# A convolution as block-Toeplitz matmuls on data reshuffled through DRAM, in a hybrid mixer and FFN trunk

## The chip, the cores and the metric

The kernel runs on the 8 cores of one Trainium2 chip. Each core takes 2 of the 16 sequences and runs both layers and the final norm on them alone; the weights are the same on all cores and no core talks to another. The time is the device time of the slowest core, in microseconds (us).

## The reference, cut to what matters

```python
# x: (16, 2048, 1024) f32; DA = DB = 384, DC = 256, CONV_WIDTH = 31, CHUNK = 128, D_FF = 2816
for l in range(2):
    h = rms_norm(x, norm1_g[l])
    z = h @ w_in[l]                                   # 1792 columns: a|gate (768), u|v (768), pool (256)
    # A: GLU, causal depthwise convolution over 31 positions, LayerNorm, silu, pointwise
    y = a * sigmoid(gate)
    y = depthwise_conv(y, conv_w[l]) + conv_b[l]      # left padding of 30
    ya = silu(layer_norm(y, conv_ln_g[l], conv_ln_b[l])) @ w_pw[l]
    # B: gated mixing of positions inside chunks of 128, 4 heads of 96 channels
    u, v = split(gelu(z_uv)); v = layer_norm(v)
    yb = u * (tril(w_s[l]) @ v + b_s[l])
    # C: trailing means over 2, 4, 8, 16 positions, minus the token, 64x64 map per group, scale
    yc = (trailing_mean(z_c, w) - z_c) @ w_pool[l] * pool_scale[l]
    x = x + concat(ya, yb, yc) @ w_out[l]
    h = rms_norm(x, norm2_g[l])
    x = x + (silu(h @ w_gate) * (h @ w_up)) @ w_down[l]
return rms_norm(x, final_g)
```

## The kernel before

The residual stream of a sequence stays in SBUF as xT, channels on partitions: 8 tiles of 128 channels by 2048 positions, f32. Work goes in four blocks j of 512 positions. Every operation is recorded by helpers of `Prog` (`mm` L343, `mms`, `transposes`, `act_op` L370, `tt` L386, `ts` L390, `stt` L397), so in the profile a line is that of a helper and a group is known by its tiles. Each engine executes its list in the order of recording and waits on semaphores where a tile's last writer or reader is on another engine.

A layer has two stages. In the **mixer**, `fa(j)` broadcasts the RMSNorm factor: `bcast_tok` (L484) makes four diagonal matrices on VectorE and multiplies ones by them in f32, and `rms_scale` (L496) writes hT, the normalised input in bf16. `fb1` and `fb2` project hT with w_in, mostly with channels on partitions, v with tokens on partitions. The convolution is split by taps: 18 taps are matmuls with diagonal matrices (`conv_pe`, 3 channel tiles times 18, each 512 columns), 6 taps are scaled by ScalarE and added by TensorE through an identity matmul, 6 are VectorE multiply-adds into acc and one a ScalarE scaling (`tap`, `tap30`). `lnv_stats` and `lnv_apply` normalise v, `pool_branch` does the trailing sums on VectorE, and the four 96-channel heads of the gating are matmuls of 128 columns. LayerNorm of the convolution takes its sums by matmuls with ones and two f32 broadcasts. The output projection (8 by 9 matmuls of 512 columns per block) is interleaved by hand with the next block's taps. `rms_tok_stats` (L460) squares on ScalarE and sums by one-column matmuls.

In the **FFN** the 22 hidden tiles go in chunks of 6, 6, 6, 4: gate and up projections from a ring of three weight slots, silu and product, then the down projection added to xT; the last chunk runs block by block and the statistics of a block are recorded after the next block's matmuls. Weights are cast from f32 to bf16 by DMAs of POOL's queue (`load_mixer_w1`, `load_mixer_wout`, `load_ring`, `load_wd`). SBUF is in regions, and `new_phase` makes all users of a region wait for all earlier ones. Between the sequences `fin_store` transposes and stores the output (four staging tiles) and `x_tr` transposes the next input.

## Time and profile before

| | us |
|---|---|
| median of 3 runs (lowest, highest) | 3571.84 (3571.19, 3571.9) |
| span of the profiled execution, slowest core | 3568.6 |
| shortest span among the 8 cores | 3562.7 |
| TensorE busy in that span | 3203.5 |
| VectorE (DVE) busy | 1693.4 |
| ScalarE (ACT) busy | 948.4 |
| GpSimd (POOL) busy | 205.0 |

The profiled execution's own time is taken as its span plus what lies around the span; the median of the runs is 3.2 us above the span. Busy time is the union of an engine's instructions. Matmuls are pipelined, so the mean duration of one (379 ns for 512 columns) is longer than the distance between two. The granted clock is the share of TensorE's full clock (2.4 GHz) that it was given in a stretch. The spans of the eight cores lie within 6 us of each other.

### The profile page before, as it was taken

To read this page: it belongs to the slowest core of one execution; us is meant where nothing else is said; L and a number is where in the kernel's file an instruction comes from. 1 tells how busy PE (TensorE), PEld (TensorE's weight loads), DVE (VectorE), ACT (ScalarE), POOL (GpSimd) and SP (SyncE) were. 2 spreads that over 40 slices of the span, in tenths; PEclk is the share of its full clock that TensorE was granted. 3 is DMA by queue.
4 is the path that set the end of the run, shared out by engine and by line. 5 is a ranking of instruction groups with operands and counts; after the bars stand their busy time and mean duration, and the time that the engine had idled before them with its cause. 6 is when DMAs were issued, how large, how long until landed. Compare 5 with 4: busy or idle time off the path is not lost.

```text
span 3568.6 us, 46876 instructions; the slowest of 8 cores (3562.7 to 3568.6 us)
## 1 busy us (share of the span) xinstructions
PE 3203.5 (90%) x15945; PEld 1564.1 (44%) x15945; DVE 1693.4 (47%) x3002; ACT 948.4 (27%) x1568; POOL 205.0 (6%) x253
## 2 busy tenths in 40 slices
PE   3799799999889879999969996999997897899997
PEld 3344344444444434444454443444443443444444
DVE  1667543323577653233356775223336765433235
ACT  3345310011344511100234552110114454101102
POOL 1000110000000010000000001000000000100000
PEclk7799889999889979999978996999997998899998
DMA  8000082120100063221150004522101000522202
GB/s 169 6 1 1 12 117 42 24 42 13 27 1 1 1 87 47 42 42 24 54 175 1 1 1 63 78 42 31 23 15 24 1 1 1 69 38 36 42 12 101
DMA packets 144642, 134.73 MB, mean 38 GB/s; under 512 B 4896, under 2 KB 120220, under 8 KB 144412
## 3 DMA queue, kind: packets, MB, share of 16 engines
q0 software_dynamic: 131008, 93.60, 19.2%
q1 hardware_dynamic: 13404, 38.14, 3.1%
q8 instruction: 135, 2.21, 0.2%
q14 instruction: 95, 0.78, 0.1%
HBM read 208.53 MB, written 16.78 MB: 63 GB/s over the span
## 4 chain that ended last, share of the span: by engine, by line
PE 80%; DVE 9%; issue 4%; ACT 4%; DMA 3%; DVEq 0%; SPq 0%; POOL 0%; ACTq 0%; POOLq 0%
PE bank L348 78%; DVE h2T L399 2%; ACT sqr_56 L377 2%; PE bank L366 1%; DVE hT L399 1%; DVE sA L387 1%; DVE acc L399 1%; PE bank L475 1%; DMA vst<-norm_g 1%; ACT sqb L377 0%; DMA out<-ostage_95 0%; DVE acc L387 0%; DVE sB L387 0%; DVE dg_60 L393 0%; ACT accb L377 0%
## 5 line engine op out<-in xcount | busy, mean ns | idle before, releaser
L348 PE MATMUL bank<-act,wd 128*128 128x512 bf16 x2816 | 632.4, 388 | 0.0
L387 DVE TENSOR_TENSOR xT<-xT,bank 128x512 f32<-128x512 f32 x640 | 439.6, 688 | 376.0 <-PE bank L348 369.0
L348 PE MATMUL bank<-h2T,ring_72 128*128 128x512 bf16 x2048 | 460.8, 388 | 31.5 <-DVE h2T L399 31.5
L348 PE MATMUL bank<-h2T,ring_73 128*128 128x512 bf16 x2048 | 444.6, 379 | 0.0
L348 PEld LDWEIGHTS bank<-act,wd 128*128 128x128 bf16 x2816 | 280.2, 100 | 345.9 <-issue 27.5
L348 PE MATMUL bank<-hT,w_in_sb 128*128 128x512 bf16 (+1 forms) x1536 | 364.6, 400 | 35.3 <-DVE hT L399 17.1
L377 ACT ACTIVATE sA<-bank 128x512 f32<-128x512 f32 x176 | 105.1, 597 | 1093.5 <-PE bank L348 1085.9
L387 DVE TENSOR_TENSOR act<-sB,bank 128x512 bf16<-128x512 f32 x176 | 121.1, 688 | 477.6 <-PE bank L348 477.6
L387 DVE TENSOR_TENSOR act<-sA,bank 128x512 bf16<-128x512 f32 x176 | 121.1, 688 | 469.3 <-PE bank L348 469.3
L348 PE MATMUL bank<-h2T,ring_74 128*128 128x512 bf16 x1536 | 333.5, 379 | 0.0
L348 PEld LDWEIGHTS bank<-h2T,ring_72 128*128 128x128 bf16 x2048 | 203.0, 100 | 286.6 <-issue 56.5
L348 PEld LDWEIGHTS bank<-h2T,ring_73 128*128 128x128 bf16 x2048 | 200.4, 98 | 241.6
L348 PEld LDWEIGHTS bank<-hT,w_in_sb 128*128 128x128 bf16 (+1 forms) x1536 | 172.0, 113 | 216.4 <-issue 66.5
L377 ACT ACTIVATE sB<-bank 128x512 f32<-128x512 f32 x176 | 105.1, 597 | 510.4 <-PE bank L348 510.4
L348 PEld LDWEIGHTS bank<-h2T,ring_74 128*128 128x128 bf16 x1536 | 150.3, 98 | 181.3
L377 ACT ACTIVATE sqr_55<-xT 128x512 bf16<-128x512 f32 x160 | 100.5, 628 | 241.6 <-PE bank L475 216.2
L348 PE MATMUL bank<-yb,wo_b 96*128 96x512 bf16 x512 | 131.6, 378 | 3.6 <-ACT ya L377 3.6
L348 PE MATMUL bank<-dg_60,onesF 128*128 128x128 f32 x256 | 76.7, 392 | 64.5 <-DVE dg_60 L393 50.3
L377 ACT ACT_TABLE_LOAD x48 | 61.6, 1283 | 259.5 <-DVE sA L387 98.4
L348 PE MATMUL bank<-ya,wo_a 128*128 128x512 bf16 x384 | 103.6, 378 | 0.0
L399 DVE SCALAR_TENSOR_TENSOR acc<-ybuf,cwT,acc 128x512 f32<-128x512 bf16 x144 | 98.9, 750 | 9.4 <-ACT acc L377 9.1
L399 DVE SCALAR_TENSOR_TENSOR acc<-ybuf_83,cwT,acc 128x512 f32<-128x512 bf16 x144 | 100.6, 750 | 4.7 <-ACT acc L377 4.6
(422 smaller groups left out, 3274.7 us busy)
## 6 DMA issues: line engine op xcount, KB each, us to landing
wd<-w_down POOLq DMA_DIRECT2D x12, 1536.0 KB, 12.1
ring_72<-w_gate_up POOLq DMA_DIRECT2D x32, 512.0 KB, 7.8
ring_73<-w_gate_up POOLq DMA_DIRECT2D x32, 512.0 KB, 7.4
w_in_sb<-w_in POOLq DMA_DIRECT2D x16, 768.0 KB, 41.3
ring_74<-w_gate_up POOLq DMA_DIRECT2D x24, 512.0 KB, 7.6
wd<-w_down POOLq DMA_DIRECT2D x4, 1024.0 KB, 8.4
out<-ostage_95 SPq DMA_DIRECT2D x8, 512.0 KB
out<-ostage_96 SPq DMA_DIRECT2D x8, 512.0 KB
```

What stands on the lines that cost most here:

```text
L348: ins = e.matmul(out, l, r, start=(first and i == 0), stop=(last and i == n - 1))
L366: ins = e.transpose(out, in_, idn)
L377: return e.activation(out=out, in_=in_, func=func, **kw)
L387: return P.add(eng, lambda e, out=out, in0=in0, in1=in1, op=op: e.tensor_tensor(out=out, in0=in0, in1=in1, op=op), reads=reads, writes=writes)
L399: e.scalar_tensor_tensor(out=out, in0=in0, scalar=scalar, in1=in1, op0=op0, op1=op1),
L475: ins = e.matmul(out, l, r, start=(k == 0 and out is mmg[0][0]), stop=(k == 7), skip_group_check=True)
```

## The change

The FFN's arithmetic stays. In the mixer and around it:

- The input of the projections is xb = x * norm1_g in bf16, without the RMSNorm factor. The projections of a, gate, u and v have tokens on partitions (384 columns each), and the factor, now one number per partition, is the scale of the operation that evicts the bank. Only the pooling branch has channels on partitions and multiplies by a broadcast factor.
- Broadcasts split the f32 factor into three bf16 parts and use three bf16 matmuls of 512 columns with ones (`split_bcast_closures`); the f32 ones go.
- The GLU output y is written to a DRAM buffer per block and read back as y2: partition (i, t) holds channel i of a group of 8 at position t of a block of 16 positions; the 128 blocks and the 48 groups lie on the free axis. The convolution is, per group of 8 channels, three matmuls of 128 columns with `toep`, the banded Toeplitz weights of the eight channels, which are expanded on the chip from `conv_t`. LayerNorm is then per partition (`lna_closures`), and f32 transposes bring the result back (`lnt`).
- In Z the window sums run on POOL, one channel tile after the other, each with a ScalarE copy of 64 partitions. The gating multiplies in 384-column matmuls, and `TR` transposes its result so that the output projection has 8 row blocks instead of 9.
- Closures for norms and LayerNorm are queued (`push`) and recorded a piece at a time (`tick`) between matmul groups, in the FFN too: there norm2 and the next layer's norm1 are recorded between the matmuls. `need` records the rest of a queue at once.
- SBUF tiles carry byte ranges instead of regions; a tile waits only for overlapping ones. The host lays out the weights and packs all vectors in one tensor, so the parameter transposes at the start go. SP has 24 DMA semaphores instead of 12.
- The final store and the next sequence's transposes are interleaved with its GLU projections; output staging has 3, then 2 tiles, and 8 at the very end.

```diff
+NI = 8
+NG = DA // NI
+ND = 3
+TB = 16
...
+    yd = [nc.dram_tensor("yd%d" % i, [S, DA], BF16, kind="Internal").ap() for i in range(2)]
...
+    def push(fn, tag=None, q=None):
+        (bg if q is None else q).append((fn, tag))
+    def pop(q):
+        fn, tag = q.popleft()
+        fn()
+        if tag is not None:
+            done.add(tag)
+    def tick(n=1):
+        for _ in range(n):
+            if bg:
+                pop(bg)
+            elif lo:
+                pop(lo)
...
+    def split_bcast_closures(s, l, j, rt, kind, sink):
+        br = B("r", kind, j)
+        bs = B("spl")
+        bd = B("dsp")
+        def split():
+            c = slice(4 * j, 4 * j + 4)
+            vec(lambda e: e.tensor_copy(out=spb[:, 0, :], in_=rt[:, c]), [br], [bs])
+            tt(spf[:, 0:4], rt[:, c], spb[:, 0, :], ALU.subtract, [br, bs], [bs])
+            vec(lambda e: e.tensor_copy(out=spb[:, 1, :], in_=spf[:, 0:4]), [bs], [bs])
+            tt(spf[:, 4:8], spf[:, 0:4], spb[:, 1, :], ALU.subtract, [bs], [bs])
+            vec(lambda e: e.tensor_copy(out=spb[:, 2, :], in_=spf[:, 4:8]), [bs], [bs])
+        def dia(i):
+            for q in range(4):
+                ts(dsp[:, i, q, :], identb[:], spb[:, i, q:q + 1], None, ALU.mult, None, [bs, bC], [bd])
+        def bc():
+            bk, bb = next_bank()
+            mm(bk[:], [(onesb[:], dsp[:, i].rearrange("p q t -> p (q t)")) for i in range(3)], [bd, bC], [bb])
+            sink(bk, bb)
+        push(split)
+        push(lambda: dia(0))
+        def dia12():
+            dia(1)
+            dia(2)
+        push(dia12)
+        push(bc, (kind + "bc", s, l, j))
...
+    def A(s, l, j):
+        need(("r1", s, l, j))
+        yt = ytok[j % 2]
+        for q in range(4):
+            tc_ = slice(q * 128, (q + 1) * 128)
+            rc = r1[:, 4 * j + q:4 * j + q + 1]
+            br = B("r", "r1", j)
+            rd = [bxb(j, k) for k in range(8)] + [w_a.b()]
+            bk, bb = next_bank()
+            mm(bk[:, 0:DA], [(xb[j][:, k, tc_], w_a[:, k, DA:2 * DA]) for k in range(8)], rd, [bb])
+            sg = sig[q % 2]
+            act_op(sg[:], bk[:, 0:DA], AF.Sigmoid, [bb, br], [sg.b()], scale=rc)
+            tick()
+            bk, bb = next_bank()
+            mm(bk[:, 0:DA], [(xb[j][:, k, tc_], w_a[:, k, 0:DA]) for k in range(8)], rd, [bb])
+            stt(yt[:, q, :], bk[:, 0:DA], rc, sg[:], ALU.mult, ALU.mult, [bb, br, sg.b()],
+                [yt.b(q, lo=768 * q, n=768)])
+            tick()
+        ydt = yd[s % 2]
+        byd = B("yd", s % 2, j)
+        dma("sync", ydt[j * NT:(j + 1) * NT, :].rearrange("(q p) c -> p q c", p=128), yt[:],
+            [yt.b(q, lo=768 * q, n=768) for q in range(4)], [byd])
+        src = ydt.rearrange("(b t) (i g) -> i t b g", t=TB, i=NI)
+        for i in range(NI):
+            dma("sync", y2[TB * i:TB * (i + 1), 2 + 32 * j:2 + 32 * (j + 1), :], src[i, :, 32 * j:32 * (j + 1), :],
+                [byd], [y2b(j)])
+    def toep_closures():
+        gs = NG // 3
+        for part in range(3):
+            for i in range(NI):
+                def f(part=part, i=i):
+                    o = toep[:, part * gs:(part + 1) * gs, :, i, :]
+                    v = vconv[:, part * gs:(part + 1) * gs, :, :]
+                    wr = [toep_b(b) for b in range(4 * part, 4 * part + 4)]
+                    if i % 2 == 0:
+                        ts(o, v, M8[:, i:i + 1], None, ALU.mult, None, [vconv.b(), bC], wr)
+                    else:
+                        act_op(o, v, AF.Copy, [vconv.b(), bC], wr, scale=M8[:, i:i + 1])
+                push(f, None, lo)
+    def conv():
+        for b in range(12):
+            bk, bb = next_bank()
+            groups = []
+            for gp in range(4):
+                g = 4 * b + gp
+                groups.append((bk[:, gp * 128:(gp + 1) * 128],
+                               [(y2[:, 2 - d:2 - d + NBLK, g], toep[:, g, d].rearrange("p i t -> p (i t)"))
+                                for d in range(ND)]))
+            mms(groups, [y2b(u) for u in range(-1, NJ)] + [toep_b(b)], [bb])
+            tt(xc[:, 32 * b:32 * b + 32, :], bk[:].rearrange("p (c t) -> p c t", t=TB),
+               cbB[:, 32 * b:32 * b + 32].unsqueeze(2).to_broadcast([128, 32, TB]),
+               ALU.add, [bb, cbB.b()], [xc_b(b)])
+            tick()
+    def lna_closures(s, l):
+        bst = [B("bna", i) for i in range(4)]
+        allx = [xc_b(b) for b in range(12)]
+        def stats(t):
+            tq, ti = t // 4, t % 4
+            vec(lambda e: e.bn_stats(out=bna[:, ti, 0:6], in_=xc[:, :, t]), allx, [bst[ti]])
+            vec(lambda e: e.bn_aggr(out=bna[:, ti, 8:10], in_=bna[:, ti, 0:6]), [bst[ti]], [bst[ti]])
...
+        def app(t):
+            ti = t % 4
+            ts(xc[:, :, t], xc[:, :, t], bna[:, ti, 8:9], bna[:, ti, 10:11], ALU.subtract, ALU.mult,
+               [bst[ti]] + allx, [B("xh", t)])
+        for tq in range(4):
+            for ti in range(4):
+                push(lambda t=4 * tq + ti: stats(t), None, lo)
+            push(fin, None, lo)
+            for ti in range(4):
+                push(lambda t=4 * tq + ti: app(t), ("lna", s, l, tq) if ti == 3 else None, lo)
+    def lnt(s, l, tq):
+        need_lo(("lna", s, l, tq))
+        for ct in range(3):
+            bk, bb = next_bank()
+            transposes([(bk[:, ti * 128:(ti + 1) * 128], xc[:, ct * 128:(ct + 1) * 128, 4 * tq + ti], identF[:])
+                        for ti in range(4)], [B("xh", 4 * tq + ti) for ti in range(4)] + [xc_b(b) for b in range(12)] + [bC],
+                       [bb])
+            dst = silT[:, ct, :].rearrange("p (b t) -> p t b", t=TB)[:, 4 * tq:4 * tq + 4, :]
+            act_op(dst, bk[:].rearrange("p (t b) -> p t b", t=4), AF.Silu, [bb, bPV],
+                   [silT.b(ct, tq, lo=4096 * ct, n=4096)], scale=pvc(l, PV_LNG + ct), bias=pvc(l, PV_LNB + ct))
+            tick()
+    def V(s, l, j):
+        rd = [bxb(j, k) for k in range(8)] + [w_uv.b()]
+        br = B("r", "r1", j)
+        for q in range(4):
+            bk, bb = next_bank()
+            mm(bk[:, 0:DB], [(xb[j][:, k, q * 128:(q + 1) * 128], w_uv[:, k, DB:2 * DB]) for k in range(8)], rd, [bb])
+            act_op(vg[:, q, :], bk[:, 0:DB], AF.Gelu, [bb, br], [vg.b(q, lo=1536 * q, n=1536)],
+                   scale=r1[:, 4 * j + q:4 * j + q + 1])
+            tick()
...
+    def SP(s, l, j):
+        for h in range(4):
+            hc = slice(96 * h, 96 * h + 96)
+            bk, bb = next_bank()
+            mm(bk[:, 0:DB].rearrange("p (q d) -> p q d", q=4), [(wsT[:, h, :], vn[:, :, hc])],
+               [vn.b(q, lo=768 * q, n=768) for q in range(4)] + [B("wsT")], [bb])
+            stt(ybt[:, :, hc], bk[:, 0:DB].rearrange("p (q d) -> p q d", q=4), pvc(l, PV_BS + h), ug[:, :, hc],
+                ALU.add, ALU.mult, [bb, bPV] + [ug.b(q, lo=768 * q, n=768) for q in range(4)], [ybt.b()])
...
+    def Zprep(s, l, j):
+        def sink(bk, bb):
+            act_op(rbc[:], bk[:], AF.Copy, [bb], [rbc.b()])
+        split_bcast_closures(s, l, j, r1, "r1", sink)
+    def Z(s, l, j):
+        need(("r1bc", s, l, j))
+        rd = [bxb(j, k) for k in range(8)] + [w_z.b()]
+        if j == 0:
+            pool(lambda e: e.memset(zc[:, :, 0:ZH], 0.0), [], [zc.b()])
+        else:
+            act_op(zc[:, :, 0:ZH], zc[:, :, NT:NT + ZH], AF.Copy, [zc.b()], [zc.b()])
+        for m in range(2):
+            bk, bb = next_bank()
+            mm(bk[:], [(w_z[:, k, m * 128:(m + 1) * 128], xb[j][:, k, :]) for k in range(8)], rd, [bb])
+            tt(zc[:, m, ZH:ZH + NT], bk[:], rbc[:], ALU.mult, [bb, rbc.b()], [zc.b()])
+            tick()
+        W = ZH + NT
+        for m in range(2):
+            zm = zc[:, m, :]
+            tt(zG[:, 1:W], zm[:, 1:W], zm[:, 0:W - 1], ALU.add, [zc.b()], [zG.b()], eng="gpsimd")
+            tt(zF[:, 3:W], zG[:, 3:W], zG[:, 1:W - 2], ALU.add, [zG.b()], [zF.b()], eng="gpsimd")
+            if m == 1:
+                tt(zG[:, 7:W], zF[:, 7:W], zF[:, 3:W - 4], ALU.add, [zF.b()], [zG.b()], eng="gpsimd")
+                tt(zF[:, 15:W], zG[:, 15:W], zG[:, 7:W - 8], ALU.add, [zG.b()], [zF.b()], eng="gpsimd")
+            act_op(zF[0:64, ZH:W], zG[0:64, ZH:W], AF.Copy, [zG.b()], [zF.b()])
+            stt(pp[:, m, :], zF[:, ZH:W], invw[:, m:m + 1], zm[:, ZH:W], ALU.mult, ALU.subtract,
+                [zF.b(), zc.b(), bC], [pp.b()])
...
+            dma("sync", sgB[:, 0, :], sg_ln_g_d[l].partition_broadcast(128), [], [sgB.b()])
+            dma("sync", sgB[:, 1, :], sg_ln_b_d[l].partition_broadcast(128), [], [sgB.b()])
+            dma("sync", cbB[:], conv_b_d[l].partition_broadcast(128), [], [cbB.b()])
+            pool(lambda e: e.memset(y2[:, 0:2, :], 0.0), [], [y2b(-1)])
+            need(("r1", s, l, 3))
+            toep_closures()
+            A(s, l, 3)
+            drain()
+            load_wo(l, 0)
+            load_wo(l, 1)
+            V(s, l, 0)
+            U(s, l, 0)
+            conv()
+            lna_closures(s, l)
+            Zprep(s, l, 0)
+            SP(s, l, 0)
+            V(s, l, 1)
+            Z(s, l, 0)
+            Zprep(s, l, 1)
+            TR(s, l, 0)
+            U(s, l, 1)
+            PM(s, l, 0)
+            SP(s, l, 1)
+            V(s, l, 2)
...
+            V(s, l, 3)
+            Z(s, l, 2)
+            Zprep(s, l, 3)
+            TR(s, l, 2)
+            U(s, l, 3)
+            PM(s, l, 2)
+            SP(s, l, 3)
+            lnt(s, l, 0)
+            Z(s, l, 3)
+            load_wo(l, 2)
+            TR(s, l, 3)
+            lnt(s, l, 1)
+            lnt(s, l, 2)
+            lnt(s, l, 3)
+            for fp in range(NRING):
+                load_ring(l, fp, fp)
+            PW(s, l, 0)
+            PM(s, l, 3)
+            load_wd(l, 0)
+            PW(s, l, 1)
+            for j in range(NJ):
+                WO(s, l, j)
+                norm2(s, l, j)
+                if j + 2 < NJ:
+                    PW(s, l, j + 2)
```

## Rows read from the trace of the kernel before

**Rows 1.** The page, busy time by engine and the chain's shares
```profile
PE 3203.5 (90%) x15945; PEld 1564.1 (44%) x15945; DVE 1693.4 (47%) x3002; ACT 948.4 (27%) x1568; POOL 205.0 (6%) x253
...
PE 80%; DVE 9%; issue 4%; ACT 4%; DMA 3%; DVEq 0%; SPq 0%; POOL 0%; ACTq 0%; POOLq 0%
```

**Rows 2.** Windows by stage: start:end, length, busy (instructions) per engine, clock, DMA share, GB/s
```profile
0.00:50.00 50.00, 27.14 (x218) 25.14 (x219) 11.55 (x22) 23.12 (x40) 8.11 (x21) 0.86 1.03 230
0.00:105.90 105.90, 35.00 (x277) 31.05 (x278) 21.93 (x48) 28.32 (x49) 16.07 (x33) 0.70 0.72 147
105.90:456.00 350.10, 302.54 (x1540) 153.65 (x1540) 233.87 (x462) 151.86 (x247) 24.28 (x27) 0.88 0.06 8
475.00:906.00 431.00, 431.00 (x1999) 195.38 (x1998) 134.63 (x196) 52.01 (x87) 18.00 (x22) 1.00 0.28 39
1779.00:1862.00 83.00, 53.41 (x465) 46.87 (x462) 43.25 (x74) 34.93 (x62) 8.41 (x11) 0.75 0.65 195
2210.00:2689.00 479.00, 469.62 (x2188) 211.88 (x2188) 164.87 (x243) 63.67 (x108) 20.03 (x24) 0.98 0.30 42
2689.00:2707.00 18.00, 6.75 (x68) 5.04 (x66) 7.34 (x18) 6.98 (x13) 4.43 (x7) 0.54 0.36 54
3533.00:3568.60 35.60, 21.64 (x176) 18.03 (x176) 23.05 (x34) 6.15 (x12) 2.01 (x2) 0.80 0.60 245
```

**Rows 3.** The chain that ended last, in time: start, length, what
```profile
81.92 1.25 DMA vst<-pool_scale
...
89.55 4.12 DMA wsst<-w_s
...
271.53 1.02 POOL bnst_63 L652
...
354.56 31.94 PE bank L348 x147
...
1805.19 15.85 DMA out<-ostage_95
```

**Rows 4.** Groups of instructions, first mixer: shapes, count | busy us, mean ns | idle before
```profile
L348 PE MATMUL bank<-w_in_sb,hT 128*128 128x384 bf16 x128 | 21.5, 326 | 0.0
...
L348 PE MATMUL bank<-sqb,identb 128*128 128x512 bf16 x36 | 13.6, 419 | 0.9 <-ACT sqb L377 0.7
```

**Rows 5.** Small matmuls: group of the whole span, timeline, group of the first mixer
```profile
L475 PE MATMUL bank<-ocS,sqr_55 128*128 128x1 bf16 x640 | 38.5, 164 | 65.0 <-ACT sqr_55 L377 63.2 <-DVE rtok L393 1.8
...
1837.76 0.71 PE L366 MATMUL bank<-ident,xT 128*128 128x128 f32 x5
...
L358 PE MATMUL bank<-wsT,vn 128*96 128x128 bf16 x64 | 8.9, 314 | 2.6 <-DVE acc L387 2.6
```

**Rows 6.** Groups of DVE and ACT, first mixer
```profile
L399 DVE SCALAR_TENSOR_TENSOR acc<-ybuf_83,cwT,acc 128x512 f32<-128x512 bf16 x36 | 25.1, 750 | 1.2 <-ACT acc L377 1.1
...
L387 DVE TENSOR_TENSOR xT<-xT,bank 128x512 f32<-128x512 f32 x32 | 21.8, 688 | 23.7 <-PE bank L348 22.5 <-PE bank L475 1.3
...
L377 ACT ACTIVATE sqr_55<-xT 128x512 bf16<-128x512 f32 x16 | 10.0, 627 | 29.0 <-PE bank L475 25.3 <-DVE xT L387 3.7
...
L399 DVE SCALAR_TENSOR_TENSOR vg<-vg,bnst_63,sgB 128x384 f32<-128x384 f32 x16 | 9.8, 613 | 5.1 <-POOL bnst_63 L652 5.1
...
L646 DVE BATCH_NORM_STATS2 bnst_62<-vg 128x6 f32<-128x384 f32 x16 | 8.9, 559 | 4.0 <-ACT vg L377 3.0
...
L377 ACT ACTIVATE sil<-sA,pv 128x512 bf16<-128x512 f32 x8 | 6.5, 814 | 3.4 <-DVE sA L387 3.3
```

**Rows 7.** DMA queues of the page (packets, MB, share of 16 engines); groups of POOL
```profile
q0 software_dynamic: 131008, 93.60, 19.2%
q1 hardware_dynamic: 13404, 38.14, 3.1%
...
L412 POOL TENSOR_SCALAR_AFFINE_SELECT ident<-onesF 128x128 f32<-128x128 f32 x1 | 0.3, 292 | 0.2 <-POOL onesF L411 0.2
...
L416 POOL MEMSET mhalf<- 128x16 f32 x1 | 0.1, 111 | 0.1
```

More of the change, by code:

```diff
@@ L1 @@
+from collections import deque
 import numpy as np
@@ L55 @@
 SEM_LIMIT = 30000
[L56 removed]
+N_DMA_SEMS = {"gpsimd": 20, "sync": 24, "scalar": 4}
 class Prog:
```

1111 lines of the change are left out of this document (492 added, 619 removed).

## The prediction

> **What bounds the kernel now.** I read the page first: TensorE (PE) is busy 90% of the span and carries 80% of the chain that ended last [rows 1]. That share averages two kinds of stage, so I cut the span at the first and last matmul of each [rows 2]. An FFN stage takes 479 us (the others are within 2 of it); in its middle TensorE is busy in 431.0 of 431.0 us at clock 1.00, 1999 recorded matmuls, 0.216 us each. A mixer stage takes 350 us (the others within 2), TensorE busy in 302.5 at clock 0.88: the granted clock is at the lower of its levels (1.2 GHz) for about a quarter of the time, after idle stretches. The start (105.9), the gaps from FFN to mixer (83 between the sequences, 18 inside the second, and 19.5 inside the first, what the rest of the span leaves) and the last store (35.6) make up the 3568.6.
>
> Inside a mixer the chain is trains of up to 32 us of matmuls, cut by pieces like the POOL power of 1.02 us for which DVE and then TensorE stand [rows 3]. So TensorE bounds the mixer, with holes where another engine must deliver. At 0.216 us per 512 columns the convolution is 3*18*4 = 216 diagonal matmuls (46.7 us) plus the 72 identity ones that add ScalarE's taps (36 of them 13.6 us, so 27) [rows 4]: 73 of the 302 us.
>
> **The change, priced per layer.** I build the new stage times instead of subtracting, because the order of work is new throughout.
>
> *GLU projections A(0..3).* 4*4*2*8 = 256 matmuls of 384 columns at 21.5/128 = 0.168 [rows 4]: 43 us, plus one block of statistics (32 at 38.5/640 = 0.060 [rows 5]), 45. DVE has per block 4 multiplies of 384 (0.62 each) and 4 of the scalings that replace hT; ScalarE 4 sigmoids, 8 squares, 4 scalings at about 0.6 [rows 6]: both under TensorE's 11 us per block. rstd is now needed by the eviction only, so the matmuls no longer wait for statistics, power, broadcast and scaling; the holes before a mixer [rows 2] go. If this cover failed, up to the 18 us of such a gap would return.
>
> *V(0), U(0)*: 64*0.168 = 11.
>
> *Reshuffle.* Each block is written to DRAM and read back by 8 DMAs on SP in pieces of 48 bf16, 96 bytes: 512 tokens * 8 = 4096 pieces, 256 for each of 16 DMA engines. No row shows such a piece. Software-queue packets average 19.2% of 16*3568.6 over 131008 = 0.084 us (714 bytes), hardware-queue ones 3.1% over 13404 = 0.13 us (2.8 KB) [rows 7]; the load of w_s (512 packets of 512 bytes, 32 per engine) holds the chain for 4.12 us against 1.25 for one of a few packets [rows 3]: (4.12-1.25)/32 = 0.09. A piece cannot be below zero; bounds 0 to 0.13. I take 0.045, half the 512-byte row, since a fifth of the bytes and the same overhead are left. Four blocks need 1024 pieces per engine and begin 14 us into the stage; the convolution is ready at 45+11 = 56. 14+46, and 4 for the last write and receipt (1.25 for a small load, two of them and the gaps), is 64: wait 8. At 0 there is none, at 0.13 it is 14+133+4-56 = 95. The Trainium skill, page "DMA: Bandwidth & Descriptors", section "Why small descriptors are slow (HBM only)", gives about 3 bus cycles of overhead beside one per 32 bytes; by that a piece is an estimated 0.01 us, there would be no wait and the sum be 32 us lower. No trace here shows it.
>
> *Convolution*: 48*3 = 144 matmuls of 128 columns, each with its own weight load. Nearest rows: 0.060 (load plus one column), f32 transposes of 128 columns (five in 0.71 with the last one's latency, so 0.106 to 0.14), the w_s matmuls 8.9/64 = 0.139 [rows 5]. Bounds 9 to 20, taken 0.10: 14. All of the 73 us of TensorE and of the tap work on DVE (72 at 0.69, 50 us [rows 6]) and ScalarE goes, so does the ybuf halo. The 24 expansions of the Toeplitz weights lie beside V(0) and U(0), 12 on each engine, 768 elements, at about the 0.7 to 0.8 of 512 f32 ones.
>
> *The V/Z/U/SP rounds.* TensorE needs V, U 192*0.168 = 32, Z 64*0.216 = 14, broadcasts 3, SP 3, bf16 transposes 48*0.106 = 5, pooling map 2: 58 for three and a bit rounds, plus 5 for the f32 transposes. DVE needs per round, by [rows 6]: V statistics and scaling 4*(0.559+0.182+0.613+0.618)+0.2+1.3 (wait for the power) = 9.4; SP 2.5; split and diagonals 0.8+3.0; Z two evictions and two differences 2.9; its part of the LayerNorm of the convolution (16 tokens of statistics 0.74 and normalisation 0.6, four powers: 27 in all, two thirds in three rounds) 6.1: 24.7. To it comes a chain in Z that the kernel before does not have: window sums on POOL (2, then 4 operations of 528 elements, f32), each set followed by a ScalarE copy, for which DVE stands with its next instruction in order; ScalarE stands too, with the evictions of U and TR behind it. POOL's 128-element one-input operation takes 0.292 against 0.111 for 16 elements [rows 7], 1.6 ns an element, so 0.95 for 528 with one input and at most double with two; I take 1.25 (bounds 0.95 to 1.9). 6*1.25 + 2*0.6 + crossings = 10.5, of which DVE works 2: 8.4 idle (bounds 6 to 12). The next V begins only after SP: 2.5 more, since TensorE with 16 of 35 us of work will be granted the lower clock much of the time, as at 2689 where it is busy 6.75 of 18.0 at 0.54 [rows 2]. A round: 24.7+8.4+2.5 = 35.6 (bounds 20, where TensorE sets it, and 45, where the clock stays low). Three rounds 107; the last Z, what is left of the normalisation (9) and 9 Silu evictions at 0.81 add 26. Together 133. The skill's page "GPSIMD Engine Reference", section 3.1, gives 2.6 cycles at 1.2 GHz for a two-input element, an estimated 1.14 us without overhead; the sum by it moves by less than 3 us per layer.
>
> *PW, WO.* 36+256+12 at 0.216 = 66, and 128 statistics at 0.060 = 8: 73 (8 row blocks instead of 9 saves 7). DVE in it: 32 adds at 0.688 and norm2 of three blocks at 10: 52; ScalarE 32 squares at 0.62: 20; both hidden. The loads of the last third of w_out and of the rings wait for Z(3) and the last transposes, issued 20 us or more before use, against 8 us to land by the page's list of DMA issues.
>
> *FFN.* 2112*0.216 = 456, 96 statistics now interleaved 6; the last block's norm2 is late by 8. 470 against 477 to 479.
>
> Layer: 45+11+8+14+133+73+470 = 754, four 3016.
>
> *Ends.* Start: the serial parameter loads, of which [rows 3] show the last but one and w_s, and their transposes go: they end at 94. A(0) needs two x blocks and w_a, 7.3 MB, at 230 GB/s [rows 2] 32 us; it then runs with 10 us of transposes between: 42 over a normal layer. Between sequences: 256 f32 transposes, 27 to 41 us by clock, and output tiles that are too few: the chain stands 15.85 us for one store [rows 3]. 60, much as before (62 more than an inner gap). End 31 (35.6 now).
>
> Sum 3016+42+60+31 = 3149, against the profiled span of 3568.6. The median of the runs, 3571.84, is 3.2 above that span, so 3152.
>
> **Rivals.**
> R1, the rounds are bound by TensorE: DVE's work spreads into neighbouring stages and POOL's chain is covered. For: DVE's average is only 47%. Against: in-order DVE stands for POOL. The 133 becomes 75: 3152-4*58 = 2920.
> R2, the 96-byte reads: at 0.084 each, 14+86+4-56 = 48 instead of 8: +160 = 3312; at 0.13, 95, +348 = 3500. For: it is the mean of the queue in this trace. Against: those packets are 7 times as large.
> R3, slower than before: the same reads at over 0.147 us a piece. 14+1024p+4-56 must exceed 8 by the 105 us per layer that the change gives (3571.84-3152 over 4); that is p = 0.147. At 0.2 the wait is 167, +636 = 3788. For: 96 bytes is far below anything measured here, 8 cores read at once. Against: every row is below 0.13.
> R4, the clock stays low and rounds cost 45: +28 a layer, with PW and the start of WO cold: 3152+4*32 = 3280.
> R5, the change does not do what it says (the Toeplitz or f32 transposes cost so much that the 73 us stay): 3152+4*55 = 3370. Against: column counts, and 0.106 us.
>
> **How the numbers follow.** Forecast 0.48, R4 0.14, R1 0.15, R2 0.14, R5 0.04, R3 0.05. A difference under 0.2% can't be told from none; no case lands there except a sliver between R2 and R3: 0.01. Faster 0.94, slower 0.05. The forecast's own range by the bounds of convolution, POOL and ends is 3080 to 3230; taking in R4, R1 and the lower half of R2: 2920 to 3370.
>
> **What would show it.** Mixer stages of about 285 us; A at clock 1.00 with TensorE 95% busy; the y2 reads landing about 12 us after issue (22 and more would be R2); in the rounds idle DVE before the pp operations, released by POOL or ScalarE, and TensorE idle before SP, released by DVE; POOL additions near 1.25 us; WO dense; FFN near 470. The forecast is wrong if the rounds show TensorE over 90% busy, if the convolution's first matmul waits over 30 us for DMA, or if WO or the FFN stops being dense because weights come late.

## The result: slower by 1.7%, and the profile after

The changed kernel takes 3630.5 us (3634.8 in a second run) beside 3571.6 for the kernel before on the same chip: ratio 1.0173, interval 1.0151 to 1.0195. My 3152 was 479 us too low, and the time lies above the range. (In some executions of either kernel one die is granted a lower clock and takes longer; such executions are left out everywhere.)

The page of after, its parts 1, 3 and 4, then the lines of part 5 that this document reads:
```profile
span 3628.2 us, 43607 instructions; the slowest of 8 cores (3613.8 to 3628.2 us)
...
PE 2787.5 (77%) x14864; PEld 1387.4 (38%) x14864; DVE 1384.3 (38%) x2657; ACT 820.5 (23%) x1240; POOL 276.7 (8%) x347
...
q1 hardware_dynamic: 87408, 49.59, 4.9%
...
PE 65%; DMA 12%; DVE 11%; issue 5%; POOL 4%; ACT 2%; DVEq 1%; SPq 0%; POOLq 0%; ACTq 0%
PE bank L326 62%; DMA y<-yd 8%; DVE dsp L371 3%; DMA yd<-ytok 2%; POOL zF L365 2%; ACT silT L355 1%; PE bank L336 1%; PE bank L344 1%; POOL zG L365 1%; DVE h2T L377 1%; DVE ybt L377 1%; DVE pp L377 1%; DVE vg L377 1%; DVE bnv L730 1%; DMA w_a_sb<-w_a 1%
...
L326 PE MATMUL bank<-dsp,onesb 128*128 128x512 bf16 x96 | 41.1, 558 | 355.3 <-DVE dsp L371 355.3
...
L336 PE MATMUL bank<-toep,y 128*128 128x128 bf16 x576 | 45.0, 253 | 196.1 <-DMA y<-yd 196.1
...
L355 ACT ACTIVATE silT<-bank,pv 128x512 bf16<-128x512 f32 x48 | 107.6, 2655 | 0.1
```
TensorE's busy time fell as planned, from 3203.5 to 2787.5 us against [rows 1], 416 less. The span grew by 60, so TensorE is idle 476 us more. The chain names the takers: DMA, 3% in [rows 1], has 12%, of which 8% are the reads of y2 (`y<-yd`), and POOL has 4%. The two releasers to look at first stand on the idle column: 355.3 us before the broadcast's matmuls (`dsp,onesb`) and 196.1 us before the convolution. 

The windows of one layer, in the columns of [rows 2], cut at A, V/U 0 and the wait, convolution, rounds with tail, PW/WO, the start of FFN, and the rest of FFN (the cut at 1321 lies 8 us inside the FFN, whose first matmul starts at 1312.5):
```profile
932.00:978.00 46.00, 44.68 (x323) 27.04 (x321) 15.45 (x31) 24.72 (x42) 2.17 (x3) 1.00 0.21 41
978.00:1045.00 67.00, 10.83 (x67) 6.31 (x65) 11.61 (x26) 13.22 (x18) 2.27 (x3) 0.60 0.34 60
1045.00:1056.30 11.30, 11.03 (x145) 11.03 (x146) 7.56 (x11) 0.00 (x0) 0.00 (x0) 0.81 0.01 1
1056.30:1227.30 171.00, 72.30 (x387) 40.99 (x385) 86.64 (x209) 58.88 (x66) 38.56 (x39) 0.70 0.06 9
1227.30:1321.00 93.70, 81.84 (x428) 36.20 (x428) 44.02 (x103) 22.86 (x40) 3.58 (x4) 0.91 0.23 41
1321.00:1360.00 39.00, 19.47 (x104) 8.53 (x105) 18.36 (x40) 6.79 (x12) 1.01 (x1) 0.78 0.00 1
1360.00:1777.00 417.00, 417.00 (x1926) 188.69 (x1925) 127.95 (x187) 50.22 (x84) 16.39 (x28) 1.00 0.26 48
```
A is as forecast. In the second window TensorE has 11 us of work in 67, in the fourth 72 in 171, with VectorE busy only 87: no engine is busy most of the time there, so waits set it; which, the experiments have to show.

The stages of all layers, cut at the first and last matmul of each in the trace (to about 2 us), summed over the four layers, beside my terms and the repaired kernel `e15_all_sp` (told below):

| us, whole program | forecast | after | error | e15_all_sp |
|---|---|---|---|---|
| A, four blocks | 180 | 179 | -1 | 179 |
| V/U 0 and wait for y2 | 76 | 238 | +162 | 67 |
| convolution | 56 | 44 | -12 | 51 |
| rounds and tail | 532 | 683 | +151 | 558 |
| PW, WO | 292 | 339 | +47 | 321 |
| FFN | 1880 | 1955 | +75 | 1897 |
| start (beyond a normal A) | 42 | 76 | +34 | 51 |
| between sequences | 60 | 84 | +24 | 73 |
| end | 31 | 30 | -1 | 29 |
| sum | 3149 | 3628 | +479 | 3226 |

**Why the convolution waits.** A stretch of the chain of waits (start, length, what) in the second window:
```profile
992.43 2.27 DMA y<-yd
994.73 0.04 issue
994.77 2.22 DMA y<-yd
...
997.44 2.58 DMA yd<-ytok
1000.05 0.03 issue
1000.08 2.21 DMA y<-yd
...
1016.94 3.44 DMA sgB<-sg_ln_g
...
1021.36 4.89 DMA yd<-ytok
1026.29 0.03 issue
1026.32 2.31 DMA y<-yd
...
1042.65 2.48 DMA y<-yd
1045.13 0.14 issue
1045.27 4.73 PE bank L336 x46
```
One read follows the other; each starts when the last has landed. In the code the eight reads of a block write eight different sets of 16 partitions but name one record, `y2b(j)`, and a writer waits for the record's last writer, here on SP. So far this is read off the code and the chain; e1 and e16 below test it. A block costs 2.6 to 4.9 us for its write and 8 times 2.2, about 20 in series, where A takes 11: the queue falls behind by 9 us a block.

**What a round is made of.** VectorE's order in the second round of the same layer (41 us, from one SP to the next); in brackets the idle time before the operation and what ended it:
```profile
1102.01 2.78 DVE L377 SCALAR_TENSOR_TENSOR ybt<-bank,pv,ug 128x384 bf16<-128x384 f32 x4 [5.09 <-PE bank L326]
...
1123.19 0.75 DVE L377 SCALAR_TENSOR_TENSOR pp<-zF,invw,zc 128x512 bf16<-128x512 f32 x1 [2.36 <-ACT zF L355]
...
1129.63 0.75 DVE L377 SCALAR_TENSOR_TENSOR pp<-zF,invw,zc 128x512 bf16<-128x512 f32 x1 [5.68 <-ACT zF L355]
...
1131.85 4.23 DVE L371 TENSOR_SCALAR dsp<-identb,spb 128x128 bf16<-128x128 bf16 x12
```
VectorE works 21.7 us of the 41. It stands 8.0 for ScalarE's copies, which follow POOL's sums, 5.0 for TensorE before it can evict the next SP's banks, 2.5 for two POOL powers, and 3.5 goes in gaps of less than 0.1 us between its 53 operations. TensorE's own 22 us of idle time before the broadcast lie beside this chain; they are its consequence.

### The profile page after: what moved, and what is told of

It is laid out like the page before. It is cut to its first block, busy times and chain, and to the rows that moved or that the text cites. A ratio compares the mean times of both kernels' runs of the same rounds, so it can differ in the third digit from the quotient of the medians.

```text
span 3628.2 us, 43607 instructions; the slowest of 8 cores (3613.8 to 3628.2 us)
## 1 busy us (share of the span) xinstructions
PE 2787.5 (77%) x14864; PEld 1387.4 (38%) x14864; DVE 1384.3 (38%) x2657; ACT 820.5 (23%) x1240; POOL 276.7 (8%) x347
## 3 DMA queue, kind: packets, MB, share of 16 engines
q1 hardware_dynamic: 87408, 49.59, 4.9%
## 4 chain that ended last, share of the span: by engine, by line
PE 65%; DMA 12%; DVE 11%; issue 5%; POOL 4%; ACT 2%; DVEq 1%; SPq 0%; POOLq 0%; ACTq 0%
PE bank L326 62%; DMA y<-yd 8%; DVE dsp L371 3%; DMA yd<-ytok 2%; POOL zF L365 2%; ACT silT L355 1%; PE bank L336 1%; PE bank L344 1%; POOL zG L365 1%; DVE h2T L377 1%; DVE ybt L377 1%; DVE pp L377 1%; DVE vg L377 1%; DVE bnv L730 1%; DMA w_a_sb<-w_a 1%
## 5 line engine op out<-in xcount | busy, mean ns | idle before, releaser
L326 PE MATMUL bank<-h2T,ring 128*128 128x512 bf16 x5632 | 1237.3, 383 | 39.4 <-DVE h2T L377 39.4
L326 PEld LDWEIGHTS bank<-h2T,ring 128*128 128x128 bf16 x5632 | 553.8, 99 | 718.4 <-issue 67.1
L365 DVE TENSOR_TENSOR act<-tsil,bank 128x512 bf16<-128x512 f32 x352 | 242.0, 688 | 973.7 <-PE bank L326 961.9
L355 ACT ACTIVATE tsil<-bank 128x512 f32<-128x512 f32 x352 | 210.1, 597 | 1588.6 <-PE bank L326 1585.5
L326 PE MATMUL bank<-dsp,onesb 128*128 128x512 bf16 x96 | 41.1, 558 | 355.3 <-DVE dsp L371 355.3
L355 ACT ACTIVATE sqr<-xT 128x512 bf16<-128x512 f32 x320 | 192.5, 623 | 205.1 <-PE bank L524 194.0
L336 PE MATMUL bank<-toep,y 128*128 128x128 bf16 x576 | 45.0, 253 | 196.1 <-DMA y<-yd 196.1
L326 PE MATMUL bank<-w_uv_sb,xb 128*128 128x384 bf16 x1024 | 193.3, 351 | 0.0
L326 PE MATMUL bank<-w_a_sb,xb 128*128 128x384 bf16 x1024 | 178.8, 331 | 1.7 <-DVE r L371 1.7
L326 PE MATMUL bank<-ya,wo 128*128 128x512 bf16 x384 | 112.9, 406 | 0.0
L326 PE MATMUL bank<-ybT,wo 128*128 128x512 bf16 x384 | 108.6, 393 | 0.0
L355 ACT ACTIVATE silT<-bank,pv 128x512 bf16<-128x512 f32 x48 | 107.6, 2655 | 0.1
```

The costliest lines, as they stand in the source:

```text
L326: ins = e.matmul(out, l, r, start=(first and i == 0), stop=(last and i == n - 1))
L336: ins = e.matmul(out, l, r, start=(i == 0), stop=(i == n - 1))
L355: return e.activation(out=out, in_=in_, func=func, **kw)
L365: return P.add(eng, lambda e, out=out, in0=in0, in1=in1, op=op: e.tensor_tensor(out=out, in0=in0, in1=in1, op=op), reads=reads, writes=writes)
```

## The experiments

Each is an edit of the changed kernel. Ratios are to the kernel before, run beside the experiment; "a layer" is the mean of the table's cuts.

**e1_reads_free.** The eight reads get records of their own.
```diff
-                [byd], [y2b(j)])
+                [byd], [y2b(j, i)])
```


> The eight reads of a block get a record of their own each, so that none waits for the one before; nothing else changes. Theory A (the reads stand in a row: each is issued when its forerunner has landed, 2.2 us a piece, 17 to 18 us a block, so the last block lands 88 us after the first is written and the convolution waits 56.4 us): the wait falls to under 10 us, the layer from 869 to about 820, between the sequences another 20 us go since the stores of the output stand behind the reads on SP, together 3630 to about 3410. Theory B (the 96-byte pieces themselves cost the time, my rival R2): a block still takes 17 us and the time stays within 1% of 3630.

3544.0, from one execution, so there is no interval. Its cores end at 3497 to 3543; the latest takes 505 us in each FFN for 489, with a granted clock of 0.81 over 60 us at its start, where TensorE is busy 19.8 or more of each 20. Why, no run here shows. Wait and V/U 0 are 22 to 27 us a layer for 47 to 67: the serial reads are the cause of most of that wait. Of the expectation (wait under 10, 3410) this falls short: the wait itself is still 12 to 17 us, and the gain is 87 us, 131 on the best core, not 220. What is left of the wait is mostly the write of the last block: it takes 11 to 14.5 us in the second layer, while the two loads of w_out recorded before it keep the DMA engines 94% busy, against a median of 3. In e15, where these loads come later, it has a median of 2.6 and the wait is 7. TensorE's wait before the broadcasts stays, 345.9 us.

**e2_reads_fat.** Reads stay serial, but each takes contiguous pieces of 3072 bytes, so y2's contents are in another order.
```diff
-            dma("sync", y2[...], src[i, :, 32 * j:32 * (j + 1), :],
+            dma("sync", y2[...].rearrange("p b g -> p (b g)"),
+                ydt[j * NT:(j + 1) * NT, :].rearrange("(i t r) c -> i t (r c)", i=NI, t=TB)[i],
```


> The eight reads of a block still wait for each other but move the same bytes in pieces of 3072 instead of 96 bytes; the convolution gets its input in a wrong order. Theory A: 2.0 to 2.2 us per read as before, wait of the convolution 50 us or more, time within 1% of 3630. Theory B: a read well under 2 us and a wait under 20 us, time 3500 or less.

3590.9 (one execution; 1.1% below 3630, where I had said within 1%); the wait with V/U 0 is still 42 to 58 us. The page's DMA line of after, of this and of e1 (KB each, median us from issue to landing):
```profile
y<-yd SPq DMA_DIRECT2D x128, 48.0 KB, 2.2
```
```profile
y<-yd SPq DMA_DIRECT2D x128, 48.0 KB, 1.8
```
```profile
y<-yd SPq DMA_DIRECT2D x128, 48.0 KB, 2.8
```
31 more pieces per DMA engine (512 pieces of 96 bytes against 16 of 3072, over 16 engines) cost 0.4 us of 2.2, so 0.013 us each; the rest is what a DMA of this size takes with long pieces too, paid eight times in series. Free of each other (third line) each takes longer, 2.8, but they overlap. So the piece was not the danger of my rivals R2 and R3.

**e3_sums_dve.** The window sums run on VectorE (`eng="gpsimd"` dropped in four places).

> The six window sums of Z per block go from POOL (1.07 to 1.3 us each) to DVE. Theory C (the chain POOL, ScalarE, DVE sets the rounds, crossings included): about 10.5 us of chain become 6 operations of 0.69 plus two ScalarE copies, 5 to 6 us less per block, 16 blocks, about 3550. Theory D (DVE's own work sets the rounds): 4 us more of it per block, 3630 to 3690.

3592.2 to 3597.6 (ratio to before 1.0062, 1.0045 to 1.0080): rounds and tail 161 a layer for 170. POOL's detour costs 9 us a layer, half of theory C and a quarter of the 38 a layer by which rounds and tail miss the forecast.

**e4_bcast_early.** The next block's broadcast is recorded whole behind Z's two evictions, ahead of the sums.
```diff
+        if j + 1 < NJ:
+            Zprep(s, l, j + 1)
+            need(("r1bc", s, l, j + 1))
         W = ZH + NT
```


> The split, the diagonals and the broadcast matmuls of block j+1 are recorded right after the evictions of Z(j), ahead of the window sums, instead of behind them. Theory E (TensorE stands 20 to 23 us per round at the broadcast matmuls in the middle of U because their diagonals are behind Z's chain in DVE's order, so U, PM, SP and V come late): the wait at the broadcast falls to about 5 us, DVE makes its 5.5 us of split and diagonals while POOL works, a round falls from 41.5 to about 34 us, three per layer, 3630 to about 3540. Theory D (DVE's sum of work sets the round): the wait moves to SP and the time falls by less than 30 us.

3620.9 to 3633.3 (ratio 1.0156, 1.0132 to 1.0179), rounds 168: 3 us a layer, although it attacks the largest line of the page. Both theories had the wait itself wrong, it stays where it was: TensorE still stands 57.1 us before the broadcasts in the second layer's rounds (68.9 in after), because V's statistics and scaling and Z's evictions stand ahead of the diagonals on VectorE, and new is a wait of 9.4 for ScalarE's `ybT`. VectorE still waits 2.95 and 5.69 us for the sums.

**e10_order.** Z(j), its evictions, POOL's sums and the next broadcast stand before V(j+1), `pp` after V's statistics; the second channel tile gets its own zF.
```diff
-            V(s, l, 1)
             Z(s, l, 0)
+            Zw1(s, l, 0)       # sums on POOL
             Zprep(s, l, 1)
+            V(s, l, 1)
+            Zw(s, l, 0)        # pp on VectorE
             TR(s, l, 0)
```


> Only the order of the rounds is changed: Z(j), its two evictions, the window sums on POOL (a second buffer zF for its second half) and the broadcast of r for the next block stand before V(j+1), pp after V(j+1)'s statistics. DVE's and POOL's work stays the same. Theory O: a round of 41.5 us is DVE's 24 us of work plus 17 us of waits in its order (POOL's sums before pp, TensorE's broadcast and evictions behind them); with the sums beside V's work the round falls to 28 to 33 us, rounds and tail from 171 to 130 to 140 a layer, and the time to 3470 to 3510. Rival C: the chain from V's matmul over its gelu, statistics, POOL's power, eight operations and SP's evictions is what sets the round, whatever stands between; it stays at 38 or more and the time at 3600 or more.

3551.8 to 3558.4 (ratio 0.9957, 0.9942 to 0.9973), below the kernel before; rounds and tail 151 a layer, 20 less. The work is the same, the order alone was worth 77 us (2.16% of 3571.6), half of what the optimistic theory said. A round takes 32 to 33 us: VectorE's waits for the sums (8.0) and for TensorE (5.0) are gone from it, and its busy time is 25.7 instead of 21.7 (why, under e20). The waits of TensorE (us in total, times, longest) of after, then of e10:
```profile
PE bank L326 <- DVE dsp L371: 355.3, 32, 23.0
```
```profile
PE bank L327 <- DVE dsp L372: 211.9, 32, 10.9
```

**e5_silt, e12_fours.** The Silu evictions of the convolution take 2.64 us each; I had 0.81. They write bf16 at a step of 32 bytes. e5 holds silT time-major, so that it is written contiguously and PW's matmuls read it with that step; e12 keeps the layout and turns the loops, to write runs of four.
```diff
-            dst = silT[...].rearrange("p (b t) -> p t b", t=TB)[:, 4 * tq:4 * tq + 4, :]
+            dst = silT[...].rearrange("p (t b) -> p t b", t=TB)[:, 4 * tq:4 * tq + 4, :]   # e5
+            dst = silT[...].rearrange("p (b t) -> p b t", t=TB)[:, :, 4 * tq:4 * tq + 4]   # e12
```


> The 12 silT evictions a layer write bf16 with a step of 32 bytes and take 2655 ns each (48 in the trace of after). Here they write contiguous runs of 128 (silT held time-major), and PW's matmuls read the strided view instead. Theory F: the time is the strided write; each falls to 0.7 to 0.9 us, ScalarE is freed 22 us a layer, the tail after the last round loses 10 to 15 of it a layer, and the time is 3570 to 3590. Rival G: the time is that of the strided PSUM source or of Silu itself; the evictions stay over 2 us and the time stays 3630. Rival H: the stride moves to TensorE, PW's 512-column matmuls grow from 0.23 to 0.4 us or more (36 a block of 512), which gives 10 to 25 us back a layer: 3630 or above.

> e5_silt moved the stride of 32 bytes from ScalarE's write (2642 ns, now 777) to TensorE's read (379 ns a matmul, now 1038) and cost 27 us a layer in PW. Here silT stays token-major, so PW reads contiguous columns again, and the eviction iterates block by block: it writes runs of four tokens (8 bytes, step 32) and reads PSUM with a step of 512 bytes. Theory: the cost of the eviction is that of each lone 2-byte write, so runs of four take 0.8 to 1.3 us, PW is back at 379 ns, the tail loses 8 to 14 us a layer and the time is 3575 to 3600. Rival: the read of PSUM with a step costs as much as the write did, the eviction stays at 2.6 us, and the time at 3630.

Instructions of tile silT (ns min/median/max) in after, e5 and e12:
```profile
L326 PE MATMUL bank<-silT,w_pw_sb x144: 379/379/634, 360.3 to 3072.8; 128*128 128x512 bf16 x144
L355 ACT ACTIVATE silT<-bank,pv x48: 2537/2642/2846, 320.1 to 3023.1; 128x512 bf16<-128x512 f32 x48
```
```profile
L326 PE MATMUL bank<-silT,w_pw_sb x144: 1017/1038/1044, 345.6 to 3154.7; 128*128 128x512 bf16 x144
L355 ACT ACTIVATE silT<-bank,pv x48: 767/777/794, 317.0 to 3085.2; 128x512 bf16<-128x512 f32 x48
```
```profile
L326 PE MATMUL bank<-silT,w_pw_sb x144: 379/379/634, 348.9 to 3023.0; 128*128 128x512 bf16 x144
L355 ACT ACTIVATE silT<-bank,pv x48: 769/777/787, 320.2 to 2975.9; 128x512 bf16<-128x512 f32 x48
```
e5: 3691.1 to 3742.1 (ratio 1.034, 1.0316 to 1.0365), 60 slower by the ratio: the step now slows 144 matmuls from 379 to 1038 ns, 26 us a layer in PW/WO, against 12 won in the tail. e12: 3582 to 3587 (ratio 1.0043, 1.0027 to 1.0059): 777 ns with runs of 8 bytes, PW as before. Reading PSUM at a step of 512 bytes costs nothing.

**e8_start.** Own records for the halves of w_a and w_uv, and the mask on wsT recorded before V(0).
```diff
-        dma("gpsimd", w_a[:, :, 0:DA], w_a_d[l, :, :, 0:DA], [], [w_a.b()])
+        dma("gpsimd", w_a[:, :, 0:DA], w_a_d[l, :, :, 0:DA], [], [w_a.b("SIB", 0)])
```


> The two halves of w_a and of w_uv get records of their own, so that POOL's queue does not wait for one half before it issues the other, and the mask on wsT is recorded just before V(0) instead of with the loads. Theory: the first norm power comes at 66 us in after because POOL stands behind these waits (24.4, 11.0 and 20.1 us in its queue); it now comes near 47, A of the first layer falls from 72 to about 52, and the time to about 3608. Rival: the first group waits for the bytes of w_a themselves, not for POOL's power; A of the first layer stays near 70 and the time at 3630.

3615.6 to 3620.2 (ratio 1.0135, 1.0115 to 1.0155), 14 less by the ratio, though the two intervals touch. The trace carries it: the first A starts 8 us earlier and takes 57 for 72, and 8 of this is given back in the wait for y2. Part of the forecast's +34 at the start.

**e18_bcast_cheap.** The broadcasts alone: 12 operations of 128 columns become 3 of 512, norm2's broadcast comes nine closures later, WO has four closures a tick instead of two.
```diff
-            for q in range(4):
-                ts(dsp[:, i, q, :], identb[:], spb[:, i, q:q + 1], None, ALU.mult, None, [bs, bC], [bd])
+            tt(dsp[:, i], identb[:].unsqueeze(1).to_broadcast([128, 4, 128]),
+               spb[:, i, :].unsqueeze(2).to_broadcast([128, 4, 128]), ALU.mult, [bs, bC], [bd])
...
-            tick(2)
+            tick(4)
```


> After with the broadcasts alone changed: the 12 diagonals as three operations of 512 columns, norm2's broadcast behind nine empty closures, four closures a tick in WO. Theory: what TensorE stands in WO and at the start of FFN (5.1, 5.1, 1.8 and then 7.3 and 5.6 us in one layer) goes, 10 to 15 us a layer from PW/WO and FFN together, nothing from the rounds: 3570 to 3590. Rival: VectorE's evictions of WO now wait behind the closures, PW/WO grows as FFN falls (as from e14_all_fours to e15_all_sp, +7 and -12): 3600 to 3615.

3520.5 and 3525.2 (ratio 0.9860, 0.9831 to 0.9889): some 108 less, twice my theory. FFN is 474 a layer for 489, PW/WO 80 for 85, and the rounds, from which I expected nothing, 162 for 170. The three parts of this edit were not separated. The large piece is FFN's start, where in after TensorE stood 7.3 us for `dsp` and 5.6 for h2T and had a clock of 0.78 in 39 us.

**All repairs.** e11_all has e1, e10, e5, e8, the cheap broadcast with nine closures and three a tick, sgB and cbB loaded ahead of the reads on SP, wo loaded after them. e13 has the old Silu eviction in its place, e14 that of e12; e15 is e14 with SP(j+1) ahead of PM(j) and four closures a tick.

> All repairs together: reads of a block free of each other, the order of the rounds of e10_order, silT written contiguous, the broadcast's 12 diagonals as three operations of 512 columns, the broadcast behind nine empty closures in WO with three a tick, own records for the weight halves, sgB and cbB loaded before the reads on SP, wo loaded after the reads. Theory (each term is a loss of its own place): -131 for the reads as the undisturbed cores of e1_reads_free had it, -120 for the rounds, -50 for silT, -25 for the broadcasts in WO and at the start of FFN, -20 for the start, sum 3280; range 3230 to 3340, below both kernels. Rival: the terms hide each other (freed ScalarE and VectorE time only moves the wait), and the kernel ends between 3400 and 3480.

> e11_all with silT evicted as in after (2-byte writes with a step of 32 bytes). PW/WO falls from the 101 to 105 us of e11_all to 80 to 84 a layer, as its 36 matmuls go from 1036 to 379 ns; the tail grows by the evictions, 8 to 13 us a layer. Theory that the two places add: 3393 - 4*22 + 4*10 = 3345. Rival, that ScalarE in the tail is now the bound (12 evictions of 2.64 us are 32 us): the tail grows by 20 or more and the time stays 3390.

> e11_all with the eviction of e12_fours. If runs of four are cheap (0.8 to 1.3 us): PW/WO at 80 to 84 us a layer and the rounds and tail at 138 as in e11_all, 3393 - 4*22 = 3305. If they cost 2.6 us, it equals e13_all_old_silu.

> e14_all_fours with SP(j+1) recorded ahead of PM(j), so that TensorE's stand for pp (14.1 us over the rounds of one layer in e11_all) lies behind the matmuls that DVE's next evictions wait for, and four closures a tick in WO, so that the last block's norm lies less in the first blocks of FFN (11.8 us for h2T and 5.4 for dsp there). Theory: -5 to -10 us a layer, 20 to 40 below e14_all_fours. Rival: pp and vn are ready within 3 us of each other on DVE, and closures run earlier only put DVE's work ahead of WO's evictions: within 10 us of e14_all_fours.

e11: 3393.2 (one execution), 113 above my sum; PW/WO at 102 to 106 a layer shows the largest part of why, e5's matmuls. e13: 3297.6 to 3299.3 (ratio 0.9240, 0.9226 to 0.9255), PW/WO 75 for 104, rounds 150 for 138: 64 less over four layers, which is what lies between it and the best cores of e11 (3362 in the profiled run). e14: 3239.3 and 3249.6, rounds 138, PW/WO 73. e13 and e14 came out 47 and some 60 below their expectations, which started from 3393 instead of 3362 and took 22 us a layer for the 29 to 31 of PW/WO. e15: 3225.2 to 3228.2 (ratio 0.9039, 0.9024 to 0.9053), some 17 below e14. The windows of e15's second layer (V/U 0, then convolution, rounds, PW/WO, FFN):
```profile
866.70:884.00 17.30, 10.56 (x68) 6.35 (x66) 6.22 (x15) 12.39 (x17) 0.00 (x0) 0.89 0.27 45
884.00:896.00 12.00, 10.90 (x144) 10.47 (x143) 9.69 (x20) 0.14 (x1) 2.21 (x4) 0.87 0.73 125
896.00:1036.40 140.40, 81.54 (x387) 43.42 (x387) 89.85 (x176) 39.13 (x66) 37.77 (x34) 0.75 0.03 5
1036.40:1116.20 79.80, 71.61 (x398) 32.78 (x397) 40.60 (x76) 21.92 (x39) 5.92 (x9) 0.97 0.38 60
1116.20:1590.70 474.50, 462.40 (x2226) 210.16 (x2224) 160.92 (x242) 69.12 (x115) 19.34 (x31) 0.99 0.29 49
```
The wait for the reads is gone (17.3 us with 10.6 of work; the other 6.7 are for ScalarE's U evictions, behind the Toeplitz expansions on that engine). In the rounds TensorE still works only 81.5 of 140.4 us.

**e16_all_serial, e17_reads_order.** e15 with the one record for the eight reads back; and after with only e1 and e10.

> e15_all_sp with one thing put back: the eight reads of a block write one record again, so that each waits until the one before has landed. Theory A (the serial reads are worth the same wherever they stand: last landing 17 to 20 us after the write of each block, the SP queue full over all four blocks of A): V0/U0 and the wait go from 15 to 17 us back to 45 to 65, and the time from 3227 to 3350 to 3400. Rival B (in e1_reads_free much of the gain was that the other loads no longer stood behind the reads on SP; with sgB and cbB ahead and wo behind, the serial reads cost less): 3290 or less.

> After with only two repairs, the free reads of e1_reads_free and the order of e10_order. If the two add, it takes off 131 (the undisturbed cores of e1_reads_free) and 79: 3630 - 131 - 79 = 3420, range 3405 to 3435. If the reads' landing and the rounds share a wait, 3450 or more.

e16: 3383.7 to 3395.3 (ratio 0.9483, 0.9454 to 0.9513): the serial reads alone cost 160 us, with the stage at 40 to 64 us a layer for 15 to 17. e17: 3433 to 3469 (ratio 0.9657, 0.9591 to 0.9722), where adding them gave 3405 to 3435. In its fastest run the cores end at 3394 to 3432, others at up to 3468, and single FFNs take 509 us for 491 as in e1. So the two roughly add; with this spread it can't be said more sharply.

**e19_all_tick4, e20_all_sums_dve.** e15 without the swap; and that with the window sums on VectorE.

> e14_all_fours with four closures a tick in WO and PM(j) left ahead of SP(j+1). In e15_all_sp both edits moved at once: rounds 138 to 139.5, PW/WO 72.3 to 79.8, FFN 486 to 474. If the tick did all of the gain, this stands 0 to 8 us below e15_all_sp (3219 to 3227); if the swap gave part of it, 5 or more above (over 3232).

> e19_all_tick4 with the ten window sums of a round... of a block (six operations of about 525 columns) on VectorE instead of POOL. In e3_sums_dve this gave 9.5 us a layer, since VectorE stood idle while POOL summed. In the new order VectorE works beside POOL, and both slow each other there (dsp 692 alone, 1.21 us beside POOL; POOL's sums 1.06 alone, 1.32 beside it). Theory 1 (VectorE is now the engine of the rounds): six operations more of 0.65 us are 3.9 us a round, rounds 138 to 148, time +30 to +45. Theory 2 (the mutual slowing costs more than it hides): the rounds stay at 138 or fall, time within 10.

e19: 3225.7 to 3257.1 (ratio 0.9072, 0.9032 to 0.9111). The times lie on both sides of my marks and decide nothing. The stages do: PW/WO and FFN together are 560 a layer in e14, 555 in e15 and 556 here, rounds 138, 139 and 138. The tick made that gain, and the swap gave none that these runs can tell. e20: 3218.0 to 3219.4 (ratio 0.9008, 0.8988 to 0.9028), the fastest kernel of this case, its interval overlapping e15's. Rounds are 133 a layer for 138 although VectorE has six operations a block more, so theory 1 falls. But PW/WO is 83 to 86 on its cores for 80 to 81, at a clock of 0.85 in the profiled core: most of the gain is lost again, and in this order POOL's help is worth little either way. What works against it: the same diagonals on VectorE, by the page of after (POOL idle beside them) and of e10 (POOL summing beside some), mean ns behind the comma:
```profile
L371 DVE TENSOR_SCALAR dsp<-identb,spb 128x128 bf16<-128x128 bf16 x384 | 97.4, 254 | 42.2 <-DVE dsp L371 3.0
```
```profile
L372 DVE TENSOR_SCALAR dsp<-identb,spb 128x128 bf16<-128x128 bf16 x384 | 139.0, 362 | 40.6 <-DVE dsp L372 1.1
```
The mean hides two kinds. In e10's trace 336 of the 384 diagonals take 254 ns as before. The other 48 started while a sum ran on POOL; they take 0.87 to 1.30 us, and every one ends 0.05 us after that sum ended. So such an operation waits for the whole sum, and a round's diagonals take 7.7 us for 4.2.

## Why the prediction was wrong, step by step

*The reshuffle's wait* (8 forecast, 49 measured a layer; +162 over the program) is the largest failed step. It failed in its form: "Four blocks need 1024 pieces per engine and begin 14 us into the stage" counts a throughput. A piece was priced too high, not too low: 4.9% of 16*3628 over 87408 packets is 0.033 us against my 0.045 and e2 shows 0.013. What I did not count was 32 reads one behind the other, at 2.2 us each: with them free the wait falls to 12 to 17 (e1), and put back into e15 they cost 160 us (e16). R2 and R3 named the stage but the wrong mechanism, and R3's condition (0.147 us a piece) never came near. That eight DMAs write one record could be read in the diff; the size of one in series could only be bounded, by 1.25 and 4.12 us in [rows 3]: 14+4*(8*1.25+2) = 62 is a wait of 6, with 4.12 in the place of 1.25 it is 98. The measured 2.2 and writes of about 3 give 14+4*(17.6+3) = 96, a wait of 40. The rule that I cited from the Trainium skill, page "DMA: Bandwidth & Descriptors", "Why small descriptors are slow (HBM only)", gave an estimated 0.01 us a piece; e2's 0.013 agrees, and it did not bear on the wait.

*A round* (35.6 forecast, 41 measured; with the tail 133 and 170 a layer, +151). Most parts were right: POOL's additions measured 1.05 to 1.3 us, 1.57 in a few (1.25 taken), VectorE's wait in Z 8.0 (8.4), its work 21.7 (24.7, of which 1.3 was a wait for a power). What failed is "The next V begins only after SP: 2.5 more": VectorE waits 5.0 for TensorE there, the second power adds 1.2, and the gaps between its short operations, 3.5 a round, were in no term. Three rounds so miss 21 us (the first takes 45). The tail misses 17, and there it is "9 Silu evictions at 0.81": 2.64 each, 16.5 us by the count and 12 by e12. The forecast took the order of the diff as given and priced its waits; e10 shows that the same work in another order is 20 us shorter, e18 that cheaper diagonals take 9 off. With e12's 12 these would make 41; together they gave 31, since e15 stands at 139. R4 expected 45 a round from a low clock. The clock was low, 0.71 in a round, but of the 5.4 us missed at most the 2.5 more before SP can be its work.

*FFN* (470 forecast, 489; +75). "The last block's norm2 is late by 8": TensorE stood 7.3 and 5.6 us for it, and the clock fell to 0.50 in the 10 us around, 0.78 over 39. With the broadcast cheap and later in the queue it is 474 (e18): the forecast's dense part was right. *PW/WO* (+47): the same broadcasts stand in WO, 5.1 and 5.1 us; 80 in e18, 73 in e14, where the norm's closures lie more in FFN. I had called all of VectorE's work there hidden.

*Start and between the sequences* (+58): POOL's queue waits between the halves of a weight and for the mask before it reaches the first power; e8 takes 23 off there, 8 of which the wait for y2 gives back. Between the sequences the SP queue's serial reads stand before the next stores and loads; A there is 103 us, 91 in e15 and 114 in e16. I had followed neither queue in order.

*Right*: A dense at clock 1.00 (44.7 a layer for 45), the convolution (11 for 14), TensorE's work as a whole, the 1.25 us on POOL, the end. No kernel here reached the forecast: with all repairs e15 is 77 us above it by the sum and e20 66. By its own marks it is wrong: the convolution's first matmul waits 56 us for DMA where it said "over 30 us". That the time fell between R2 and R3 (3312 and 3788) is no merit of either. What the range lacked was a rival in which the mixer is a chain of latencies; 48% on a sum that took nearly every wait between engines as hidden was the error of judgement.

## What to carry to other kernels

Where a change splits one transfer into several, look at what each waits for before pricing its bytes: DMAs that share a record land one after another, at about 2.2 us each here. The largest line of idle time names where the wait shows, not what moves it: recording that work earlier gave 3 us a layer (e4), reordering the producer's whole chain 20 (e10). So follow the engine that is waited for, operation by operation, over one round, and add up its idle time by what ended it. A stride that hurts a writer may hurt the reader more; look for the loop order in which neither steps, before changing the layout.
